# Sample sparse attention: four places instead of two for the keys of the pages and the recent keys

## The reference, cut to what matters

```python
o_cmp, p_cmp = cmp_branch(q, qpos, ctx['ck'], ctx['cv'], ctx['c_end'], table)
idx = select_blocks(p_cmp, qpos, ctx['n_slc'])
o_slc = slc_branch(q, qpos, idx, ctx['fetch'], table)
o_win = win_branch(q, q_pos0, ctx['wkv'], ctx['wpos0'], table)
o = gates[:, :, 0] * o_cmp + gates[:, :, 1] * o_slc + gates[:, :, 2] * o_win
```

## Time and profile before

| | us |
|---|---|
| median of 3 runs | 3344.78 |
| lowest, highest | 3342.7, 3346.07 |
| the profiled execution, its own time | 3348.81 |
| its span | 3347.0 |
| TensorE clock granted, mean over the span | 0.947 of full |

### The profile page before, as it was taken

One profiled execution on the slowest core, in us unless ns is written; L12 is line 12 of the kernel. 1 busy time (PEld: TensorE's weight loads), 2 busy tenths in 40 slices (PEclk: granted clock), 3 DMA queues, 4 the chain that ended last, 5 costly groups with the idle time before them and its releaser, 6 DMA issues.

```text
span 3347.0 us, 49333 instructions
## 1 busy us (share of the span) xinstructions
PE 3070.3 (92%) x19991; PEld 2876.7 (86%) x19991; DVE 1266.8 (38%) x1979; ACT 978.6 (29%) x1657; POOL 343.4 (10%) x342
## 2 busy tenths in 40 slices
PE   5999959989999999999888688988789999999999
PEld 5999838889999999998787577776379999999999
DVE  5112753443322323342031677775054332232332
ACT  4212414332211111131323576664042321111110
POOL 0000120000100101000000243442000100000010
PEclk8999979899999999999889698998889999999999
DMA  4110043011111111112400000001321111111113
GB/s 147 57 45 20 1 146 127 26 38 44 50 46 49 42 53 44 41 47 75 142 32 20 1 1 1 1 1 59 94 82 38 44 50 45 44 49 46 48 45 129
DMA packets 64341, 173.37 MB, mean 52 GB/s; under 512 B 7473, under 2 KB 28095, under 8 KB 63055
## 3 DMA queue, kind: packets, MB, share of 16 engines
q1 hardware_dynamic: 49512, 153.18, 13.8%
q10 hardware_dynamic: 14664, 17.90, 1.7%
HBM read 157.25 MB, written 17.99 MB: 52 GB/s over the span
## 4 chain that ended last, share of the span: by engine, by line
PE 71%; DVE 6%; ACT 3%; issue 2%; DVEq 2%; SPq 2%; DMA 1%; POOL 0%; POOLq 0%; ACTq 0%
PE ps L348 58%; PE ps L2396 1%; PE ps L1880 1%; PE ps L2353 1%; PE ps L2340 1%; PE ps L1453 1%; PE ps L2695 1%; PE ps L2342 1%; SPq L1850 1%; DVE jf L2507 0%; SPq L1851 0%; PE ps L1175 0%; PE ps L1420 0%; DVEq L2262 0%; PE ps L1446 0%
## 5 line engine op out<-in xcount | busy, mean ns | idle before, releaser
L348 PE MATMUL ps<-h_hi,w_hi 128*128 128x344 f32 x3360 | 727.3, 325 | 50.4 <-DVE h_lo L407 12.1
L348 PE MATMUL ps<-h_lo,w_hi 128*128 128x344 f32 x3360 | 720.7, 323 | 0.0
L348 PE MATMUL ps<-h_hi,w_lo 128*128 128x344 f32 x3360 | 716.4, 322 | 0.0
L348 PEld LDWEIGHTS ps<-h_hi,w_hi 128*128 128x128 f32 x3360 | 572.7, 190 | 58.3 <-issue 45.2
L348 PEld LDWEIGHTS ps<-h_lo,w_hi 128*128 128x128 f32 x3360 | 575.8, 191 | 0.0
L348 PEld LDWEIGHTS ps<-h_hi,w_lo 128*128 128x128 f32 x3360 | 567.1, 190 | 0.0
L300 DVE TENSOR_TENSOR w_lo<-w_raw,w_hi 128x1024 fp32r<-128x1024 f32 (+1 forms) x202 | 302.7, 1500 | 299.6 <-ACT w_hi L294 299.4
L294 ACT ACTIVATE w_hi<-w_raw 128x1024 fp32r<-128x1024 f32 (+1 forms) x202 | 208.5, 1033 | 491.0 <-PE ps L348 431.0
L1653 POOL TENSOR_TENSOR f_silu<-f_silu,nb_r 128x1032 f32<-128x1032 f32 x44 | 106.6, 2423 | 1756.2 <-ACT f_silu L1617 1756.2
L1575 DVE TENSOR_TENSOR xT<-xT,ps 128x1032 f32 (+1 forms) x64 | 78.7, 1229 | 448.9 <-PE ps L348 448.9
L348 PE MATMUL ps<-hid_hi,w_hi 128*128 128x344 f32 x1056 | 223.9, 320 | 0.0
(11 more groups left out here) (496 smaller groups left out, 3676.1 us busy)
## 6 DMA issues: line engine op xcount, KB each, us to landing
w_raw<-w_gu SPq DMA_DIRECT2D x88, 512.0 KB, 3.6
w_raw<-w_dn SPq DMA_DIRECT2D x32, 448.0 KB, 3.2
w_raw<-w_a SPq DMA_DIRECT2D x27, 512.0 KB, 3.7
xT<-xT SPq DMA_DIRECT2D x2, 4128.0 KB, 16.0
w_raw<-w_o SPq DMA_DIRECT2D x16, 512.0 KB, 3.7
w_raw<-w_dn SPq DMA_DIRECT2D x16, 512.0 KB, 3.7
pages<-cmp SPq DMA_DIRECT2D x64, 128.0 KB, 2.5
w_raw<-w_b SPq DMA_DIRECT2D x9, 512.0 KB, 3.6
```

The costliest lines, as they stand in the source:

```text
L348: mm = pe.matmul(ps[:, 3 * slot + c, 0:cut], w[:, slot, k * P:(k + 1) * P], a[:, k, c * cut:(c + 1) * cut], start=(k == 0 and w is w_hi an ...
```

## The change

The keys of the pages and the recent keys get four places, `b % 4`, in place of two. Four places of page keys fill the 16 KB of `w_hi` and `w_lo` exactly; `kTw` grows from 4 KB to 8 KB per partition. The guard is now "from `b = 4` on, wait until sample `b - 4` is scored". The eight page transfers and the recent keys of a sample count on one semaphore, one for each place, so PE waits once for 9 transfers in place of once for 8 and once for 1. All instructions of all engines, 4788 on PE and 628 on SP in the compiler's lists, stand in the order they had; only the waits attached to them differ.

```diff
         def k_of(b, pg):
-            return (w_hi_at - vs_at) // 4 + (b % 2) * SEQ + pg * P
+            return (w_hi_at - vs_at) // 4 + (b % 4) * SEQ + pg * P
...
-        kTw = pack(t_at, "kTw", [P, 2, 512])
+        assert w_hi_at + 4 * 4 * SEQ <= w_hi_at + 16 * DM
+        kTw = pack(t_at, "kTw", [P, 4, 512])
...
-        y_ld, y_k, y_v, y_w = sem("y_ld"), [sem("y_k0"), sem("y_k1")], sem("y_v"), [sem("y_w0"), sem("y_w1")]
+        y_ld, y_v = sem("y_ld"), sem("y_v")
+        y_k = [sem("y_k0"), sem("y_k1"), sem("y_k2"), sem("y_k3")]
...
             for b in range(NB):
-                if b >= 2:
-                    sp.wait_ge(y_s, b - 1)
+                if b >= 4:
+                    sp.wait_ge(y_s, b - 3)
                 snsa_pages(sp, b, 0)
-                sp.dma_start(kTw[:, b % 2, :], A["win_k"][b]).then_inc(y_w[b % 2], 16)
+                sp.dma_start(kTw[:, b % 4, :], A["win_k"][b]).then_inc(y_k[b % 4], 16)
...
-                eng.dma_start(page_to(b, pg), A["slc"][v]).then_inc(y_k[b % 2], 16)
+                eng.dma_start(page_to(b, pg), A["slc"][v]).then_inc(y_k[b % 4], 16)
...
-                pe.wait_ge(y_k[b % 2], 16 * 8 * (b // 2 + 1))
-                pe.wait_ge(y_w[b % 2], 16 * (b // 2 + 1))
+                pe.wait_ge(y_k[b % 4], 16 * 9 * (b // 4 + 1))
...
-                pe.matmul(ps[0:R, 3, :], qz12[:, b, :], kTw[:, b % 2, :], start=(b == 0), stop=False).then_inc(y_s, 1)
+                pe.matmul(ps[0:R, 3, :], qz12[:, b, :], kTw[:, b % 4, :], start=(b == 0), stop=False).then_inc(y_s, 1)
...
             def pages(b):
-                if b >= 2:
-                    act.wait_ge(y_s, b - 1)
+                if b >= 4:
+                    act.wait_ge(y_s, b - 3)
                 snsa_pages(act, b, 1)
```

## The result

| | before | changed |
|---|---|---|
| median, us (20 runs each) | 3347.11 | 3335.03 |
| lowest to highest, us | 3341.85 to 3353.32 | 3329.33 to 3345.88 |
| profiled execution, its own time, us | 3348.81 | 3334.43 |
| its span, us | 3347.0 | 3332.6 |

The ratio is 0.9967, with a 95% interval of 0.9959 to 0.9975: 11 us faster, between 8.4 and 13.7. The difference of the medians is 12.1 us.

The account below looks back on a forecast made before the run. The prediction took the kernel to be bound by a two-place ring through SP's issuing, landing and PE's scoring. An earlier end of the scores saved 10.1 us, other terms 0: 3344.78 - 10.1 = 3334.7 us, range 3330 to 3340.

Parts of the forecast that it names:

- What bounds the kernel: Samples' stage: PE's score products and SP's queue wait for each other over two key places; guard's price 9.5 us.
- SP's list: SP's issuing in the samples' stage: steps of 6.0 us, sample 7's first page at 2358.9, its recent keys at 2363.4.
- ACT's list: ACT's issuing behind the compressed softmax: start 1.0 us later, steps 5.8 us, sample 7 at 2360.1, finishing together with SP's issuing.
- The end of the scores: PE starts sample 7, the last, at 2367.6 instead of 2377.68, which saves 10.1 us.
- PE: Last sample's three score products: speed left as it is, 0, with bounds of 0.6 us lost and 1.9 us won.
- PE never holds the ring: Three score products take 2.6 us at full clock, 5.1 at half, both under the 6.0 us between samples.
- The merged semaphore: One PE wait fewer for each sample: 0, bounded by the 0.14 us between landing and start.
- Behind the scores: Masks, softmax and value products after the scores: 0, with 2.5 us either way if the clock rises earlier or later.
- Bandwidth: Loads of the samples' stage: 262 GB/s asked, 81 to 88% of what the DMA engines can do; the main unknown.
- The rival: Transfers become the bound in the samples' stage: engines sustain 236 GB/s, 5.5 us saved, 3339.3 us; chance 0.10.
- The sum: Whole kernel: median before, 3344.78, less 10.1 us gives 3334.7 us, 0.30% faster.
- the bounds: Saving: 11.3 us with steps 5.88, landing 3.5; 8.4 with 6.30 and 4.4; with the clock's, 5.3 to 15.7 us.

Follow-up runs that it names:

- values after the scores: Changed kernel, with SP issuing the recent values of all samples only once sample 7 is scored; ratio to before 0.9966.
- merged semaphore: Kernel before, two places and old guard, with only the recent keys counted on the pages' semaphore so PE waits once; ratio 1.0003.
- fixed pages: Changed kernel, with page numbers known at compile time (pages 0 to 63) in place of those of the table; ratio to before 0.9936.
- early numbers: Changed kernel, SP reading numbers of pages 0 to 4 of all samples into registers while idle and issuing those five, ACT three; ratio 0.9941.
- the fastest version: Changed kernel, SP reading its page numbers into registers while idle, ACT issuing all recent values after the last pages; ratio 0.9928, median 3322.94 us.

## Why the prediction was right

- **What bounds the kernel.** Right: a ring of two places that turns through SP's issuing, a landing and PE. Old guard with four places, ratio 0.9998; new guard with three, 0.9973.
- **SP's list.** Sample 7's first page was put at 2358.9; counted from S as in the trace of before it came at 2358.6 (2357.49 + 1.08). Step 5.95 against 6.0 us.
- **ACT's list.** Two small misses in the same direction: it starts 0.3 us behind the softmax, not 1.0, and steps in 5.7 us, not 5.8, so sample 7's pages come at 2358.8, 1.3 us before the 2360.1 forecast. "The two lists finish together" was wrong by about that much: SP's recent keys are what PE waits for. The run with values after the scores, whose ACT list is shorter still, had PE on sample 7 only 0.3 us earlier. There SP's list ended 1.0 us later, counted from S, and the keys landed in 2.9 us in place of 4.2.
- **The end of the scores.** PE on sample 7 at 2367.6 forecast, 2367.3 measured (2366.24 + 1.08): 10.4 us saved against 10.1. The recent keys landed in 4.2 us, inside the 3.5 to 4.4.
- **PE.** Taken as 0 with bounds of -1.9 and +0.6; the pair of traces shows -1.5, so the bias product L2675 came at 2370.3 (2369.18 + 1.08), not near 2372. The other runs hold 2.8 us with two places (merged semaphore) and 4.4 with four (old guard), so the number of places does not decide it. What the rows do show is the wait in front: in the three traces with a slow last sample PE had waited 2.1, 2.3 and 6.1 us for it, in the ten others 1.8 us or less. The wait's length alone is no rule either, since sample 5 of the changed kernel ran at the full clock behind a wait of 3.3 us. So it stays open whether these 1.5 us belong to the change. "PE never holds the ring" was closer than forecast: sample 6 ran at the half clock (0.50 from 2361 to 2366) and ended only 0.3 us before sample 7 could start, where a wait of 1 to 3.5 us had been forecast. The group of products that starts cold after a wait, as the Trainium skill tells it ("TensorE: Matmul & The Clock Gate", section "HAM oscillation — how this bites in real kernels"), is seen in some of these traces and not in others: of the changed kernel's six samples behind a wait, two started at the half clock.
- **The merged semaphore.** Forecast 0, measured 1.0003 [0.9994, 1.0012].
- **Behind the scores.** Taken as 0 with 2.5 us to each side; 0.8 us won in this pair, by a rise of the clock within the first sample's products.
- **Bandwidth.** The rival did not come: 267 GB/s were held for 24 us at a share of 0.87, and fixed pages drew 311 GB/s. The Trainium skill's rule beside that rival ("DMA: Bandwidth & Descriptors", section "Issuing engines are not separate DMA queues"), that issuing from several engines saves only sequencer time, usually small beside the transfer, does not hold here: issuing took 5.9 us for 1.573 MB, the transfers 5.1 at 311 GB/s, and early numbers brought PE to sample 7 7.1 us sooner.
- **The sum.** 3334.7 forecast, 3335.03 measured, and the agreement to 0.3 us is luck. The forecast stood on a median of 3 runs, 3344.78; over 20 runs before is at 3347.11, 2.3 us higher. Against that the saving is 12.1 us by medians, 2.0 more than the 10.1 forecast, and the two misses cancel. The mechanism is no luck: the saving is 11.0 us by the ratio, and its interval of 8.4 to 13.7 holds the forecast.
- **A slip in the bounds.** Six steps of 6.30 us, 4.49 us and a landing of 4.4 us put the data at 2369.6, not 2369.2, and the saving at 8.0 us, not 8.4. It changes nothing above.

## What to carry to other kernels

When a place is free again only after the work that fills the engine, the depth of the ring, the issuing and the transfers do not add: more depth gave 11 us, cheaper issuing 4 alone, both together 21. So price a guard by the longest of what runs once it is gone (here issuing, 5.9 us a sample, then the transfers, 5.1), and do not expect cheaper issuing to pay while the guard holds. Find the bound anew after each step: in the fastest version it was the queue that still read its page numbers late. Read numbers that are known early into registers while the queue stands idle, and do not put a burst of transfers that can wait right in front of the one that ends the chain.

## What the runs showed of the hardware

- A page transfer with its number read from a table costs SP's queue 1.3 us (5.95 us for four and a plain transfer); with a number known at compile time 0.7 (2.59 us for four), and with one read early also about 0.7 (3.59 us for five).
- With fixed pages, transfers of 128 KB and 256 KB reached 311 GB/s over 24 us (share 1.06), while their median landing on SP's queue rose from 2.9 to 5.4 and from 4.0 to 6.7 us, against the changed kernel at 267 GB/s: a landing read where transfers come singly can't be used where they come in a burst.
- The same three products took 2.7 to 5.0 us in different traces, by the granted clock, and the stage began up to 7 us apart (2309.95 to 2316.89). Two traces can differ by most of what this change is worth. The starts counted from one row within the stage repeat better: 51.6 to 52.3 us for the changed kernel, three places and values after the scores, whose stages begin 3.1 us apart.
